# One step of the attention pipeline, three VectorE jobs in another order

## The chip, the cores and the metric

The kernel runs on one core of a Trainium2 chip. The metric is the device time of one execution in microseconds. Three runs of the kernel before took 2973.51, 2974.47 and 2975.86 us; the median is 2974.47.

## The reference, cut to what matters

The reference is four transformer layers on one sequence of 512 tokens, model width 1024, in float32: two layers of a first block and two of a second block. The change touches the second block alone. Each of its layers has two attentions over 8 heads of 64, computed in blocks of 128 queries:

```python
# fox_attention: causal, with a decay from summed forget gates
s = einsum('bhqd,bhkd->bhqk', qi, k) * scale + ci[..., :, None] - c[..., None, :]
p = softmax(where(kpos <= qpos, s, -inf)); o = einsum('bhqk,bhkd->bhqd', p, v)
# nsa_attention: compressed keys (o_c), selected keys (o_s), window keys (o_w), two groups of four heads
o_n = g[..., 0:1] * o_c + g[..., 1:2] * o_s + g[..., 2:3] * o_w
```

With 512 tokens the selection takes all key blocks, so o_s and o_w are two plain causal attentions with different keys and values. Around the attentions stand the projections of the layer (w_in, w_o_fox, w_o_nsa, w_out) and an MLP.

## The kernel before, in words

**Five programs.** Each engine has a program of its own, written by a function (`tensor_program`, `scalar_program`, `vector_program`, `sync_program`, `gpsimd_program`). They meet only at semaphores. An engine executes its instructions in the order in which its program issues them; nothing reorders them later.

**Weights.** They come in units of up to 128x1024. SyncE loads a unit into `RAW`, ScalarE copies its upper part into `Wh` (line 1412), VectorE subtracts to get the lower part `Wl` (line 2110), and TensorE multiplies with three products, upper by upper, upper by lower, lower by upper (lines 643 to 645). `Wh` and `Wl` are made two units ahead, at the moment when a program calls `next_unit`.

**Attention beside projections.** The attentions are generators ("sides"). The projection loops call `tick()` after each few matmuls, and each tick lets every open side do one step. All engine programs tick in the same places, so that step i of an attention stands at the same place of each program's order.

**A step.** The function `mixing` exists in the TensorE, ScalarE and VectorE programs. An item is one query block t of one head; there are 32 items in a fox layer and 64 in an nsa layer, 192 in all. Its scores are 128 rows by 128, 256, 384 or 512 columns. In step i:
- TensorE: `turn(i-3)` transposes item i-3's normalised exponents (line 858, waits for `norm`), then `head(i)` computes item i's scores (lines 921, 922, 924, 917), then, every second step, `mix` multiplies a pair with the values (lines 879, 880).
- ScalarE: `turn(i-3)` copies the turned exponents' upper part into `PTh` (line 1458), then `head(i)` takes the exponential with the sum (line 1592), which waits for item i's maximum.
- VectorE: `turn(i-3)` subtracts for the lower part `PTl` (`lower`, line 2158), which waits for ScalarE's upper part; `invert(i-1)` inverts a sum (line 2394), which waits for ScalarE's exponential of i-1; `head(i)` takes the maximum (line 2389), which waits for item i's scores.
- GpSimd: multiplies the exponents of an item by the inverse (line 3157), which waits for `invert`; TensorE's `turn` two steps later waits for this.

Every score tile and every turned tile has one of the 8 PSUM banks, handed out in rotation. A score's bank is free after the exponential, a turned tile's after VectorE's `lower`, an output's after `add_up` (lines 2854 and 2866), which follows a ScalarE copy (lines 1894, 1902) that stands behind the exponential of its step.

The evacuations of the projections (lines 2247, 2249, 2814, 3040) stand between the steps in VectorE's and ScalarE's order.

Of the kernel before, what the change touches and what calls it, by code (L numbers as in the profile page):

```python
# [586 lines left out]
def norm_of(block, l, place):  # L587
    return 4 * block + 2 * l + place
# [1501 lines left out]
def vector_program(ve, M, G, K, plan):  # L2090
# [63 lines left out]
    def lower(lo, src, h, gain=None):  # L2154

        ve.wait_ge(*hi.due())
        if gain is None:
            return ve.tensor_tensor(lo, src, h.bitcast(F32), ALU.subtract)  # L2158
        return ve.scalar_tensor_tensor(lo, src, gain, h.bitcast(F32), ALU.mult, ALU.subtract)  # L2159
# [222 lines left out]
    def mixing(B, group=False, add_up=None, finish=None, need=None, tail=7):  # L2382
        tag, items = B.tag, B.items

        def head(i):
            t, g, h = items[i]
            name = f"{tag} s{i}"
            ve.wait_ge(*K.full(name))
            ve.tensor_reduce(M.STT[:, 0, t, h:h + 1], M.bank[K.of(name)][:, 0:len(B.blocks(i)) * P], AX.X, ALU.max, negate=True).then_inc(*mx.up())  # L2389

        def invert(i):
            t, g, h = items[i]
            ve.wait_ge(*K.drained(f"{tag} s{i}"))
            ve.reciprocal(M.STT[:, 4, t, h:h + 1], M.STT[:, 1, t, h:h + 1]).then_inc(*rec.up())

        def turn(i):
            name = f"{tag} t{i}"
            lower(B.turned(M.PTl, i), M.bank[K.of(name)][:, 0:len(B.blocks(i)) * P].rearrange("p (k c) -> p k c", c=P),
                  B.turned(M.PTh, i)).then_inc(*K.empties(name))

        n = len(items)
        for i in range(n + tail):
            if group and i < n and (i == 0 or items[i][1] != items[i - 1][1]):
                while (tag, items[i][1]) not in done:
                    yield
            c = B.ended(i - 5)
            if need and c is not None and B.closes(c) and items[i - 5][0] in PAIRS[1]:
                while need not in done:
                    yield
            if 0 <= i - 3 < n:  # L2410
                turn(i - 3)
            if 0 <= i - 1 < n:
                invert(i - 1)
            if i < n:
                head(i)
            if c is not None and B.closes(c):
                done.add(B.outs[c])
            c = B.ended(i - 6)
            if c is not None and B.closes(c):
                add_up(*items[i - 6])  # L2420
            c = B.ended(i - 7)
            if finish and c is not None and B.closes(c):
                finish(*items[i - 7])
            yield
# [273 lines left out]
    for l in range(DEPTH):  # L2698
        n = norm_of(0, l, 0)
# [50 lines left out]
    for l in range(DEPTH):  # L2750
        n = norm_of(1, l, 0)
# [117 lines left out]
        def fox_side():  # L2869
            yield from idle(FOX_WAIT)  # L2870
            yield from mixing(fox_bundles(l), True, fox_sum, fox_out)
# [15 lines left out]
        def nsa_side():  # L2887
            while fox in sides.open:
                yield
            yield from blocks_side()  # L2890
            done.add(("blocks", l))
            while ("keys", l) not in done:
                yield
            q4 = M.QNS[:, :, :].rearrange("p a (h d) -> p a h d", d=64)
            tm = [M.RT[:, i, :].rearrange("p (a h b) -> p a h b", h=8, b=8) for i in range(4)]
            for s in range(NT):
                ve.wait_ge(*K.drained(f"qn{l} {s}"))
            rope(q4[:, :, :, 0:8], q4[:, :, :, 8:16], (over(nco, 8, 2), over(nsi, 8, 2), over(nsi, 8, 2), over(nco, 8, 2)), tm).then_inc(G.rq, 1)
            yield
            for j in range(2):  # L2900
                k4 = M.KST[:, :, j, :].rearrange("p a (h d) -> p a h d", d=64)
                tm = [M.RT[:, i, 0:64].rearrange("p (a h b) -> p a h b", h=2, b=8) for i in range(4)]
                if j == 0:
                    for s in range(NT):
                        ve.wait_ge(*K.drained(f"ks{l} {s}"))
                    ve.wait_ge(G.rq, l + 1)
                else:
                    ve.wait_ge(G.rk, 2 * l + 1)
                rope(k4[:, :, :, 0:8], k4[:, :, :, 8:16], (over(nco, 2, 2), over(nsi, 2, 2), over(nsi, 2, 2), over(nco, 2, 2)), tm).then_inc(G.rk, 1)
                yield  # L2910
            yield from idle(2)
            for j in range(6):
                yield from heads_side(j)
            yield from idle(5)
            yield from mixing(nsa_bundles(l), add_up=nsa_sum, need=("compressed", l), tail=6)
# [312 lines left out]
```

## Time and profile before

| what | us |
|---|---|
| median of three runs | 2974.47 |
| the profiled execution's own time | 2974.36 |
| its span, first to last instruction | 2972.6 |
| TensorE matmuls busy in it | 2786.2 (94%) |
| VectorE busy | 1497.9 (50%) |
| ScalarE busy | 1215.4 (41%) |
| GpSimd busy | 131.9 (4%) |
| mean granted TensorE clock | 0.973 of full |

Times in the profile are microseconds from the span's start, unless marked ns. A row that ends in [x <-Y] says that the engine sat idle for x before the instruction, until Y had ended. The steps of `mixing` lie in four stretches: fox about 1268 to 1385 and 2150 to 2270, nsa about 1434 to 1638 and 2316 to 2520.

### The profile page before, as it was taken

To read this page: it belongs to the slowest core of one execution; us is meant where nothing else is said; L and a number is where in the kernel's file an instruction comes from. 1 tells how busy PE (TensorE), PEld (TensorE's weight loads), DVE (VectorE), ACT (ScalarE), POOL (GpSimd) and SP (SyncE) were. 2 spreads that over 40 slices of the span, in tenths; PEclk is the share of its full clock that TensorE was granted. 3 is DMA by queue.
4 is the path that set the end of the run, shared out by engine and by line. 5 is a ranking of instruction groups with operands and counts; after the bars stand their busy time and mean duration, and the time that the engine had idled before them with its cause. 6 is when DMAs were issued, how large, how long until landed. Compare 5 with 4: busy or idle time off the path is not lost.

```text
span 2972.6 us, 34957 instructions
## 1 busy us (share of the span) xinstructions
PE 2786.2 (94%) x13625; PEld 2286.9 (77%) x13625; DVE 1497.9 (50%) x2695; ACT 1215.4 (41%) x2169; POOL 131.9 (4%) x221
## 2 busy tenths in 40 slices
PE   7999999998999999979889999999979888999998
PEld 6777888886778888767667888888767677888886
DVE  6755433357543434656655553343656655543343
ACT  4553222245432223455656343232445655342231
POOL 1000000000000000011111000000010111000000
PEclk9899999999999999989999999999989999999999
DMA  4102332330123323212211223332212211233332
GB/s 127 40 25 86 99 98 94 98 89 26 38 87 100 97 95 100 81 37 71 79 36 43 86 91 100 94 97 93 81 36 85 65 36 43 93 100 99 95 97 78
DMA packets 186359, 231.42 MB, mean 78 GB/s; under 512 B 11874, under 2 KB 140356, under 8 KB 186196
## 3 DMA queue, kind: packets, MB, share of 16 engines
q1 hardware_dynamic: 184500, 225.95, 24.2%
q0 software_dynamic: 976, 1.32, 0.3%
q8 instruction: 109, 1.79, 0.2%
q10 hardware_dynamic: 720, 1.92, 0.2%
q14 instruction: 54, 0.44, 0.0%
HBM read 227.05 MB, written 2.11 MB: 77 GB/s over the span
## 4 chain that ended last, share of the span: by engine, by line
PE 74%; DVE 13%; ACT 7%; issue 4%; DMA 0%; POOL 0%; ACTq 0%; DVEq 0%; SPq 0%; POOLq 0%
PE bank L643 22%; PE bank L645 22%; PE bank L644 22%; DVE Wl L2110 2%; ACT Wh L1412 2%; DVE PT L2158 2%; DVE STT L2389 1%; PE bank L803 1%; ACT P L1592 1%; ACT PT L1458 1%; PE bank L858 1%; PE bank L879 1%; PE bank L740 1%; DVE KAl L2814 1%; PE bank L1103 1%
## 5 line engine op out<-in xcount | busy, mean ns | idle before, releaser
L2110 DVE TENSOR_TENSOR Wl<-RAW,Wh 128x1024 fp32r<-128x1024 f32 (+3 forms) x434 | 511.2, 1200 | 396.3 <-ACT Wh L1412 395.4
L1412 ACT ACTIVATE Wh<-RAW 128x1024 fp32r<-128x1024 f32 (+3 forms) x434 | 438.1, 1032 | 367.9 <-PE bank L645 367.4
L643 PE MATMUL bank<-Hh,Wh 128*128 128x512 f32 (+1 forms) x976 | 395.5, 405 | 9.1 <-DVE Wl L2110 7.5
L645 PE MATMUL bank<-Hh,Wl 128*128 128x512 f32 (+1 forms) x976 | 385.2, 395 | 0.0
L644 PE MATMUL bank<-Hl,Wh 128*128 128x512 f32 (+1 forms) x976 | 385.0, 394 | 0.0
L643 PE MATMUL bank<-Wh,A 128*128 128x512 f32 x864 | 337.2, 390 | 0.0
L645 PE MATMUL bank<-Wh,A 128*128 128x512 f32 x864 | 336.2, 389 | 0.0
L644 PE MATMUL bank<-Wl,A 128*128 128x512 f32 x864 | 336.2, 389 | 0.0
L643 PE MATMUL bank<-HA,Wh 128*128 128x512 f32 x704 | 276.7, 393 | 7.2 <-DVE HA L2159 7.2
L645 PE MATMUL bank<-HA,Wl 128*128 128x512 f32 x704 | 275.5, 391 | 0.0
L644 PE MATMUL bank<-HA,Wh 128*128 128x512 f32 x704 | 275.3, 391 | 0.0
L643 PEld LDWEIGHTS bank<-Hh,Wh 128*128 128x128 f32 (+1 forms) x976 | 185.4, 190 | 50.2 <-DVE Wl L2110 8.4
L645 PEld LDWEIGHTS bank<-Hh,Wl 128*128 128x128 f32 (+1 forms) x976 | 184.4, 189 | 41.8
L644 PEld LDWEIGHTS bank<-Hl,Wh 128*128 128x128 f32 (+1 forms) x976 | 184.8, 189 | 34.9
L643 PE MATMUL bank<-Wh,Hh 128*128 128x512 f32 (+2 forms) x512 | 207.1, 405 | 4.3 <-DVE Wl L2110 2.7
L645 PE MATMUL bank<-Wh,Hl 128*128 128x512 f32 (+2 forms) x512 | 195.2, 381 | 0.0
L644 PE MATMUL bank<-Wl,Hh 128*128 128x512 f32 (+2 forms) x512 | 194.5, 380 | 0.0
L1592 ACT ACTIVATE P<-bank,STT 128x384 f32<-128x384 f32 (+1 forms) x192 | 101.4, 528 | 219.5 <-DVE STT L2389 219.3
L645 PEld LDWEIGHTS bank<-Wh,A 128*128 128x128 f32 x864 | 162.2, 188 | 33.7
L644 PEld LDWEIGHTS bank<-Wl,A 128*128 128x128 f32 x864 | 162.2, 188 | 33.3
L643 PEld LDWEIGHTS bank<-Wh,A 128*128 128x128 f32 x864 | 162.2, 188 | 33.3
L2158 DVE TENSOR_TENSOR PT<-bank,PT 128x384 fp32r<-128x384 f32 (+1 forms) x192 | 93.9, 489 | 169.2 <-ACT PT L1458 168.4
(371 smaller groups left out, 4440.8 us busy)
## 6 DMA issues: line engine op xcount, KB each, us to landing
RAW<-in_w_up_dram SPq DMA_DIRECT2D x108, 512.0 KB, 3.7
RAW<-in_w_down_dram SPq DMA_DIRECT2D x108, 512.0 KB, 3.8
RAW<-in_w_in_dram SPq DMA_DIRECT2D x90, 512.0 KB, 3.5
RAW<-in_w_gate_dram SPq DMA_DIRECT2D x44, 512.0 KB, 3.5
RAW<-in_w_out_dram SPq DMA_DIRECT2D x28, 512.0 KB, 3.8
RAW<-in_cmp_w_dram SPq DMA_DIRECT2D x16, 512.0 KB, 3.9
RAW<-in_w_o_fox_dram SPq DMA_DIRECT2D x8, 512.0 KB, 3.4
RAW<-in_w_o_nsa_dram SPq DMA_DIRECT2D x8, 512.0 KB, 3.4
```

Of the source, the lines that this page charges most:

```text
L643: pe.matmul(o, sh, mh, start=first, stop=False)
L644: pe.matmul(o, sh, ml, start=False, stop=False)
L645: return pe.matmul(o, sl, mh, start=False, stop=last)
L740: i = pe.transpose(b[:, s * P:(s + 1) * P], M.X[:, s, k * P:(k + 1) * P], ident)
L803: x = pe.matmul(b[:, h * 64:(h + 1) * 64], M.PT[:, i % 3, k * P:(k + 1) * P], values(g, h, kb[k]), start=k == 0, stop=k == len(kb) - 1)
L858: x = pe.transpose(b[:, k * P:(k + 1) * P], e[:, k * P:(k + 1) * P], ident)
L879: pe.matmul(b[:, c:c + w], v, ph, start=B.opens(n) and k == 0, stop=False, skip_group_check=True)
L1103: pe.matmul(b[:, 0:w], M.MQ[0:96, h, t * P:w], M.MK[0:96, h, 0:w], start=True, stop=True)
L1412: sc.activation(M.Wh[:, v % NHL, 0:n], M.RAW[:, v % NRAW, 0:n], ACT.Copy).then_inc(G.w_hi, 1)
L1592: sc.activation(e, M.bank[K.of(name)][:, 0:e.shape[1]], ACT.Exp, bias=M.STT[:, 0, t, h:h + 1], accum_out=M.STT[:, 1, t, h:h + 1]).then_inc ...
L2110: ve.tensor_tensor(M.Wl[:, v % NRAW, 0:n], M.RAW[:, v % NRAW, 0:n], M.Wh[:, v % NHL, 0:n].bitcast(F32), ALU.subtract).then_inc(G.w_lo, 1)
L2158: return ve.tensor_tensor(lo, src, h.bitcast(F32), ALU.subtract)
```

## The change

VectorE's `mixing` issues the three jobs of a step in another order. Before: lower part of item i-3, inverse of item i-1, maximum of item i. After: maximum of item i, inverse of item i-1, lower part of item i-3. Instructions, operands, waits and the other engines' programs stay as they are; both attentions of both layers of the second block use the function.

```diff
@@ vector_program, mixing, the loop over steps
             if need and c is not None and B.closes(c) and items[i - 5][0] in PAIRS[1]:
                 while need not in done:
                     yield
+            if i < n:
+                head(i)
+            if 0 <= i - 1 < n:
+                invert(i - 1)
             if 0 <= i - 3 < n:
                 turn(i - 3)
-            if 0 <= i - 1 < n:
-                invert(i - 1)
-            if i < n:
-                head(i)
             if c is not None and B.closes(c):
                 done.add(B.outs[c])
```

## Rows read from the trace of the kernel before

**Rows 1.** Windows: start:end, length, busy us (count), clock, DMA share, GB/s.

```profile
1434.00:1638.00 204.00, 173.72 (x993) 139.31 (x991) 107.84 (x277) 118.12 (x258) 38.98 (x64) 0.95 0.14 42
2150.00:2270.00 120.00, 98.13 (x530) 77.95 (x529) 67.62 (x144) 60.54 (x136) 19.53 (x32) 0.91 0.14 43
```

**Rows 2.** TensorE's waits, 1434 to 1638 (nsa): total us, times, longest.

```profile
PE bank L858 <- POOL P L3157: 13.2, 9, 2.7
PE bank L1285 <- DVE CB L2986: 5.2, 2, 3.3
PE bank L858 <- DVE ONS L2866: 4.4, 3, 2.0
PE bank L921 <- DVE PT L2158: 3.6, 3, 1.8
```

**Rows 3.** TensorE's waits, 2150 to 2270 (fox).

```profile
PE bank L858 <- POOL P L3157: 8.7, 2, 7.3
PE bank L879 <- DVE OAy L2854: 4.8, 2, 4.4
PE bank L858 <- DVE OAy L2854: 4.7, 1, 4.7
PE bank L921 <- DVE OAy L2854: 3.7, 3, 1.3
```

**Rows 4.** ScalarE's longest wait, 1434 to 1638.

```profile
ACT P L1592 <- DVE STT L2389: 68.0, 54, 2.7
```

**Rows 5.** The chain that ended last, by line, 1434 to 1638.

```profile
by line: issue 13.4%; DVE PT L2158 8.0%; DVE Wl L2110 6.3%; DVE STT L2389 6.0%; ACT Wh L1412 5.7%; ACT P L1592 5.3%; PE bank L643 5.1%; ACT PT L1458 4.9%; PE bank L645 4.6%; PE bank L644 4.5%; PE bank L858 3.5%; ACT L1592 3.5%; PE bank L879
```

**Rows 6.** One line's instructions each: durations ns min/median/max, starts, forms.

```profile
L2389 DVE TENSOR_REDUCE STT<-bank x192: 270/470/692, 1271.6 to 2516.3; 128x1 f32<-128x384 f32 x48, 128x1 f32<-128x512 f32 x48, 128x1 f32<-128x128 f32 x48, 128x1 f32<-128x256 f32 x48
L2158 DVE TENSOR_TENSOR PT<-bank,PT x192: 279/487/693, 1282.0 to 2520.0; 128x384 fp32r<-128x384 f32 x48, 128x512 fp32r<-128x512 f32 x48, 128x128 fp32r<-128x128 f32 x48, 128x256 fp32r<-128x256 f32 x48
L2394 DVE RECIPROCAL STT<-STT x192: 150/153/164, 1277.1 to 2518.1; 128x1 f32<-128x1 f32 x192
```

**Rows 7.** Timeline of an nsa step: start, duration, engine, line, operands, [idle <-releaser].

```profile
1483.18 0.23 PE L917 MATMUL bank<-CMB,IDB 128*128 128x128 bf16 x1
1483.26 0.60 ACT L1458 ACTIVATE PT<-bank 128x512 fp32r<-128x512 f32 x1 [0.88 <-PE bank L858]
1483.89 0.69 DVE L2158 TENSOR_TENSOR PT<-bank,PT 128x512 fp32r<-128x512 f32 x1 [0.44 <-ACT PT L1458]
1484.57 0.27 DVE L2389 TENSOR_REDUCE STT<-bank 128x1 f32<-128x128 f32 x1
1484.87 0.37 ACT L1592 ACTIVATE P<-bank,STT 128x128 f32<-128x128 f32 x1 [1.02 <-DVE STT L2389]
1486.93 0.33 PE L858 MATMUL bank<-CST,P 128*128 128x128 f32 x1 [1.55 <-DVE ONS L2866]
```

**Rows 8.** Timeline of a step behind a weight subtraction.

```profile
1465.93 1.23 DVE L2110 TENSOR_TENSOR Wl<-RAW,Wh 128x1024 fp32r<-128x1024 f32 x1 [1.77 <-ACT Wh L1412]
1467.07 0.68 DVE L2158 TENSOR_TENSOR PT<-bank,PT 128x512 fp32r<-128x512 f32 x1
1468.52 0.45 PE L858 MATMUL bank<-CST,P 128*128 128x128 f32 x1 [2.66 <-POOL P L3157]
```

**Rows 9.** Timeline around a fox output's wait.

```profile
1294.84 0.48 PE L921 MATMUL bank<-KAh,QA 128*128 128x512 f32 x1
1296.66 0.68 DVE L2249 SCALAR_TENSOR_TENSOR TQ<-bank,RBB 128x512 f32<-128x512 f32 x1
1299.74 0.67 DVE L2389 TENSOR_REDUCE STT<-bank 128x1 f32<-128x512 f32 x1
1302.48 0.58 PE L879 MATMUL bank<-PT,VF 128*128 128x256 f32 x1 [4.40 <-DVE OAy L2854]
```

**Rows 10.** ScalarE's exponentials ahead of the 4.7 us wait of the second fox stage.

```profile
2207.65 0.58 ACT L1592 ACTIVATE P<-bank,STT 128x384 f32<-128x384 f32 x1 [1.28 <-DVE STT L2389]
2210.83 0.69 ACT L1592 ACTIVATE P<-bank,STT 128x512 f32<-128x512 f32 x1 [1.02 <-DVE STT L2389]
```

## The prediction

> **What bounds the kernel now.** I read four views. The windows first, for the stretches in which the changed steps run [rows 1]: columns are TensorE matmul and weight load, VectorE, ScalarE and GpSimd busy. In the 204 us of an nsa stage TensorE is busy 173.7 us, VectorE 107.8 and ScalarE 118.1, and the granted clock is 0.95; in 120 us of a fox stage TensorE is busy 98.1 and the clock is 0.91. So TensorE is not full here, though it is 94% busy over the span, and the two other engines together are busy for about one stage length: they could do their work side by side easily, but if they take turns they fill the stage.
>
> The waits come second. TensorE waits in the nsa stage for GpSimd's multiply (13.2 us), for `add_up` (4.4), for a turned tile's bank (3.6) and for the compressed branch (5.2) [rows 2]; with five smaller groups (3.4 together) that is 29.8 us. In the fox stage it is 21.9 us [rows 3]. Both layers: about 103 us, of 2972.6.
>
> Third, who makes these late: ScalarE's exponential waits for VectorE's maximum 54 times in one nsa stage, 68.0 us in all, 1.26 us each [rows 4]. The chain of the stage [rows 5] confirms it: VectorE's lower part has 8.0% of it, 16.3 us, the maximum 6.0%, the exponential 5.3%, the upper part 4.9%. That is the taking of turns: upper part (ScalarE), lower part, inverse, maximum (VectorE), exponential (ScalarE), then whatever ScalarE has next. Elsewhere in the kernel the chain lies on matmuls, and this change does not reach it.
>
> **The change part by part.** Nothing is added or removed; 192 steps get another order on VectorE. No DMA is in these steps, and GpSimd, SyncE and TensorE keep their order. The medians are 0.47 us for the maximum, 0.49 for the lower part, 0.15 for the inverse, of which 0.07 passes before the next starts; for the same tile the maximum and the lower part cost nearly the same, 0.27 to 0.69 us [rows 6].
>
> (a) *The maximum goes ahead.* In the step of [rows 7] the scores' last matmul ends at 1483.41, ScalarE's upper part at 1483.86, and the maximum starts only at 1484.57, behind the lower part that waited for the upper one. In the new order the maximum runs 1483.45 to 1483.75, beside the upper part; the exponential follows the upper part at 1483.9 instead of 1484.87. That is 0.97 us less, and the ScalarE copy of the output, the next `Wh`, the `Wl` that waits for it, and `add_up` all come 0.9 us sooner. TensorE's wait of 1.55 us at 1486.93 would be about 0.65. This is a step in which VectorE keeps up with TensorE. Where VectorE is behind by a step, the whole idle time before the exponential (1.0 to 1.6 us) can go.
>
> (b) *Behind a `Wl`.* In [rows 8] VectorE comes from a weight subtraction and everything is ready. Before: lower part 0.68, inverse, GpSimd, transpose. After: maximum 0.67 in its place, then the inverse. The inverse gains nothing, and TensorE's 2.66 us wait shrinks only by what came before the `Wl`. Its exponential does gain the lower part and the inverse, 0.75 us.
>
> (c) *The lower part goes last.* It starts later by the maximum and the inverse, 0.47 + 0.07 = 0.54 us at the median, unless it had to wait for ScalarE anyway. Queued behind it are only the projection evacuations. Who waits for it: `mix`, two steps on, which has room, and the reuse of its PSUM bank. TensorE waited for that bank three times in the nsa stage, 3.6 us [rows 2]; I let all three grow by 0.54, 1.6 us per layer.
>
> (d) *The inverse behind the maximum.* Where a fox stage starts, TensorE waits 7.3 us for item 0 [rows 3]; item 0's inverse now stands behind item 1's 512-wide maximum, 0.67 us. TensorE waits that much more, but this does not set the later end: VectorE's and ScalarE's own order, which the 4.4 us wait hangs on, is not shifted. Price 0; 0.7 per layer if I am wrong.
>
> *The nsa stage summed.* I walked the chain from one matmul event to the next and gave each section either the amounts of (a) and (b) or the TensorE waits in it, whichever is less (they are the single entries of the groups in [rows 2]; times are ends of sections). To 1445: one step as in (a), 1.0. To 1468: waits of 1.1, 1.8 and 2.7; a `Wl` step's 0.75 on its way to the exponential, a step as in (a), and 0.5 at a 128-wide step, 2.2. To 1478: 0.2. From 1483 to 1502: no matmul at all in the chain, waits of 1.6, 1.7, 0.4 and 0.5 us, of which 3.5 can go. To 1527: 2.3, the rest being table loads of ScalarE, which stay. To 1543: 0.9. From there to 1638: 4.2 us of waits that hang on a step, take 3.2; the compressed branch's 5.2 us stay. Sum 13.3, below the 16.3 us that the lower part has in the chain. Minus (c), 1.6: 11.7 us per layer. The ends for this term: -1.6 (nothing of (a) arrives) and 24.6 (29.8 of waits less the 5.2).
>
> *The fox stage summed.* In [rows 9] the scores of 512 are issued at 1294.84, but VectorE reaches their maximum at 1299.74: it is a step behind. The projection's tile `TQ` is handled at 1296.66; with the two idle spans before it gone VectorE is free for it when TensorE has it, about 1295.0, which is 1.65 sooner; the 512-wide maximum then stands ahead of a 0.29 us lower part, so 1.95 us of the 4.40 us wait go. Before the 4.7 us wait two exponentials sit idle for 1.28 and 1.02 us [rows 10], both in steps where VectorE is behind: 2.3 us. The three waits of about 1.2 us for a score's bank [rows 3] lie in steps where the maximum has to wait for the scores anyhow: 0. Sum 4.2 us per layer. Ends: -0.7 (d), and 9.1, the two waits.
>
> *The clock.* At 0.95 and 0.91 the two stretches lose some 10 us each to a granted clock below full [rows 1], and the matmuls behind a wait run at the lower of the two levels. The waits shrink by 15.9 of 51.7 us, a third; a third of the 20 us would be 6, but part of it lies where TensorE waits anyway. I take 1.4 us per layer, ends 0 and 6.
>
> Sum: 2 x (11.7 + 4.2 + 1.4) = 34.6 us. The profiled execution took 2974.36, which is the median of the runs (2974.47) within 0.1, so the forecast is 2940.
>
> A rule that speaks against all of this: the Trainium skill, page "Perfetto Trace Analysis", section "Identifying the Most-Contended Engine", says to find the engine with the highest occupancy and to work on that one first. By it TensorE at 94% is the engine, VectorE at 50% is not, and a reordering on VectorE is worth 0. The trace bears it out for the span, not for these stretches, where TensorE's share is 82 to 85%.
>
> **The rivals.**
> *No change (2974).* TensorE is the bound, and each wait that goes comes back at the next table load, `Wl` or bank. For it: 94% busy; ScalarE's table loads and the `Wl` steps of (b), where the inverse gains nothing. Against: 68 us of exponentials waiting in one stage, and a chain that leaves TensorE for 18 us at a time.
> *Half of it (2958).* The waits for GpSimd, 13.2 us of the 29.8, hang on the inverse, which (b) does not speed up; if most of these steps start with a `Wl` the nsa term is about 5 and the fox term 2: 2 x (5 + 2 + 0.7) = 15 to 16 us.
> *More (2918).* Once ScalarE and VectorE work side by side they never fall behind, and nearly all step waits go: 2 x (20 + 6 + 2) = 56.
> *Slower (2980).* The maximum waits for scores, and VectorE is in order: while it waits, a ready inverse and a ready lower part stand behind it. Where TensorE is itself held at the scores for a bank (PT, ONS, OAy, P: 3 + 3 + 3 + 1 times per layer or so), the bank it wants next comes free later by 0.54 us or more, and so on at each such place. It decides if VectorE is seldom behind TensorE. 10 places x 0.54 x 2 layers = 11, less a few us of (a): +6. Against it: 54 of the 64 exponentials of an nsa stage waited for the maximum [rows 4], and in [rows 7, 9] the scores were there first.
> *It doesn't do what it says.* The order in a step could be masked by the waits themselves: if the scores always landed later than the lower part ended, old and new would be the same. Against it: [rows 7, 9] show scores that lay ready; this is part of "no change".
>
> **Chances.** Forecast (2926 to 2951) 0.57, half of it 0.17, more 0.12, no change 0.07, slower 0.07. The likeliest gives 2940. The range reaches to the half case and most of the "more" case: 2920 to 2965. A measurement of this kernel tells 0.2%, about 6 us, from no change. Faster by over that: 0.85, same 0.08, slower 0.07.
>
> **What would show it.** Right: ScalarE's wait for the maximum falls from 68 us in an nsa stage to under 25; the chain's share of the lower part falls from 8% to under 3%; TensorE's waits for GpSimd and `add_up` in the nsa stage fall from 17.6 to under 9; the 4.4 and 4.7 us waits of fox to about 2.4 each; the 7.3 us wait grows to about 8. The first block and the MLPs keep their times. Wrong: TensorE's waits for PT's bank grow past 6 us per nsa stage, or VectorE sits idle before the maximum for scores longer than ScalarE sat before, or the clock of the stretches stays and eats the gain.

## The result and the profile after

The changed kernel took 2933.7 us (median of four runs, 2932.05 to 2935.11) against 2973.99 for the kernel before (2973.43 to 2975.86): ratio 0.9863, 95% interval 0.9846 to 0.9880, 40.3 us less. The profiled execution took 2932.05 us with a span of 2930.2, 42.4 us less than the span of before; it was the fastest of the four runs. The same 34957 instructions ran; TensorE's matmuls were busy 2775.1 us (95%), VectorE 1503.6 (51%), ScalarE 1216.8 (42%).

Where in the kernel it was gained is read from instructions that both traces have. The first block ends within 0.3 us of before. The first transposes of nsa's queries (line 932) mark the end of the fox stage, and the sums split for the output projection (`MXl`, line 2158, first and last of 16) come behind the nsa stage of either layer. One line from each kernel's record of line 932, the kernel before first; the two times in each are those of the first and the last start:

```profile
L932 PE MATMUL bank<-CST,QNS x32: 270/272/329, 1405.3 to 2299.0; 128*128 128x128 f32 x32
```

```profile
L932 PE MATMUL bank<-CST,QNS x32: 270/272/328, 1398.8 to 2271.0; 128*128 128x128 f32 x32
```

At 1405.3 the changed kernel is 6.5 us ahead, at 2299.0 28.0 us. Line 2158 of the kernel before, then of the changed one:

```profile
L2158 DVE TENSOR_TENSOR MXl<-M,MXh x16: 691/693/694, 1664.3 to 2568.6; 128x512 fp32r<-128x512 f32 x16
```

```profile
L2158 DVE TENSOR_TENSOR MXl<-M,MXh x16: 692/693/693, 1642.7 to 2526.3; 128x512 fp32r<-128x512 f32 x16
```

Here it is 21.6 and 42.3 us ahead. So the four stages gave 6.3 (fox), 15.1 (nsa), 6.5 (fox) and 14.3 us (nsa), and nothing came from elsewhere.

The stretches of the changed kernel as windows, columns as in [rows 1]: nsa of layer 0, fox of layer 1. Each reaches some 4 to 6 us further into the work than its window in [rows 1], so it holds more matmuls.

```profile
1427.00:1622.00 195.00, 176.61 (x1026) 143.00 (x1025) 113.11 (x282) 121.71 (x263) 39.18 (x64) 0.96 0.16 47
2128.00:2246.00 118.00, 100.32 (x549) 80.56 (x548) 72.06 (x147) 63.13 (x139) 19.57 (x32) 0.94 0.15 49
```

TensorE is busy for 91% of the nsa window, where it was 85% in [rows 1]; with the end of the window moved to the same work (1427.4 to 1616.8, 995 matmuls, 171.0 us busy) it is 90%. Its waits there, the answer to [rows 2]:

```profile
PE bank L858 <- POOL P L3157: 8.0, 4, 3.4
PE bank L1285 <- DVE CB L2986: 4.2, 2, 2.5
PE bank L921 <- DVE PT L2158: 3.2, 3, 1.9
PE bank L858 <- DVE ONS L2866: 1.7, 2, 1.2
```

GpSimd's 13.2 us became 8.0 and `add_up`'s 4.4 became 1.7. The turned tile's bank stayed near its 3.6. In the fox stage, the answer to [rows 3]:

```profile
PE bank L858 <- POOL P L3157: 8.1, 1, 8.1
PE bank L921 <- DVE OAy L2854: 3.7, 3, 1.3
PE bank L858 <- DVE OAy L2854: 3.1, 1, 3.1
PE bank L879 <- DVE OAy L2854: 2.8, 1, 2.8
```

The start of the stage waits 8.1 us instead of 7.3, the two output waits fell from 4.7 and 4.4 to 3.1 and 2.8, the three short ones did not move. ScalarE's waits of the nsa stage, the answer to [rows 4], and VectorE's:

```profile
ACT P L1592 <- DVE STT L2389: 34.8, 38, 2.7
ACT PT L1458 <- PE bank L858: 32.8, 21, 4.5
```

```profile
DVE STT L2389 <- PE bank L917: 29.8, 19, 5.2
DVE Wl L2110 <- ACT Wh L1412: 18.3, 15, 2.5
DVE PT L2158 <- ACT PT L1458: 11.4, 14, 1.6
```

The exponential's wait for the maximum halved, from 68.0 us to 34.8. What is new is that ScalarE's upper part waits for TensorE's transposes (32.8 us, 15.3 before), and VectorE's maximum for TensorE's scores (29.8 us; no such wait was in the trace of before). Both engines are now up with TensorE in more of the steps and wait for it there. The chain of the same window, the answer to [rows 5]:

```profile
by line: issue 9.9%; PE bank L643 9.1%; PE bank L645 8.2%; PE bank L644 8.1%; PE bank L858 5.4%; DVE Wl L2110 5.2%; DVE STT L2389 4.9%; ACT Wh L1412 4.5%; PE bank L879 3.6%; ACT P L1592 3.5%; PE bank L921 3.0%; PE bank L880 2.9%; PE bank L9
```

The lower part (8.0% in [rows 5]) is no longer among the lines shown, the last of which has 2.9%; the three matmul lines have 25.4% where they had 14.2% (24.7% with the window ended at 1617, at the same work).

The step of [rows 7], in the changed kernel:

```profile
1472.27 0.23 PE L917 MATMUL bank<-CMB,IDB 128*128 128x128 bf16 x1
...
1472.35 0.60 ACT L1458 ACTIVATE PT<-bank 128x512 fp32r<-128x512 f32 x1 [2.10 <-PE bank L858]
...
1472.54 0.29 DVE L2389 TENSOR_REDUCE STT<-bank 128x1 f32<-128x128 f32 x1
...
1472.86 0.37 ACT L1592 ACTIVATE P<-bank,STT 128x128 f32<-128x128 f32 x1
1472.98 0.69 DVE L2158 TENSOR_TENSOR PT<-bank,PT 128x512 fp32r<-128x512 f32 x1
...
1474.92 0.33 PE L858 MATMUL bank<-CST,P 128*128 128x128 f32 x1 [0.45 <-DVE ONS L2866]
```

The maximum runs while ScalarE still makes the upper part. From the upper part's start to the exponential's start it is 0.51 us; in [rows 7] it was 1.61. TensorE's wait for the output behind it is 0.45 us instead of 1.55. The step of [rows 8], behind a `Wl`:

```profile
1455.74 1.23 DVE L2110 TENSOR_TENSOR Wl<-RAW,Wh 128x1024 fp32r<-128x1024 f32 x1 [2.02 <-ACT Wh L1412]
1456.88 0.68 DVE L2389 TENSOR_REDUCE STT<-bank 128x1 f32<-128x512 f32 x1
1457.48 0.15 DVE L2394 RECIPROCAL STT<-STT 128x1 f32<-128x1 f32 x1
...
1458.34 0.30 PE L858 MATMUL bank<-CST,P 128*128 128x128 f32 x1 [3.41 <-POOL P L3157]
```

From the start of `Wl` to TensorE's transpose it is 2.60 us, 2.59 in [rows 8]: the maximum took the lower part's place, and the wait grew from 2.66 to 3.41 because TensorE came to it earlier. The exponential, though, started 1.86 us behind the start of `Wl` instead of 2.52. Three waits of this kind (2.0, 3.4 and 1.7 us) are most of what is left of GpSimd's 8.0.

The gain can be split once more. Between the same instructions of both traces (borders at 1270.8, 1405.3, 1664.3, 2152.0, 2299.0 and 2568.6 before, at 1270.6, 1398.8, 1642.7, 2130.5, 2271.0 and 2526.3 after; what lies between the third and the fourth border belongs to no stage), TensorE's waits can be summed, and its busy time can be compared, as the number of matmuls is the same to within one:

| stage | gain, us | TensorE's waits, before and after | TensorE busy, before and after |
|---|---|---|---|
| fox, layer 0 | 6.3 | 21.9, 17.6 | 111.5, 109.4 |
| nsa, layer 0 | 15.1 | 33.5, 21.5 | 226.2, 223.2 |
| fox, layer 1 | 6.5 | 23.1, 18.9 | 124.0, 121.7 |
| nsa, layer 1 | 14.3 | 31.0, 20.4 | 238.2, 234.5 |

The waits shrank by 31.1 us and the busy time by 11.1, together the 42.2 us of the four stages. Over the whole kernel the busy time fell by the same 11.1 us (2786.2 to 2775.1) for 13625 matmuls in both, and the mean granted clock rose from 0.973 to 0.977. So about a quarter of the gain is TensorE doing the same work faster; that this is the clock, and not partly the modelled ends of single matmuls, is an estimate that the clock's mean supports.

### The profile page after: what moved, and what is told of

Same layout as the page of the kernel before. It is cut to its first block, busy times and chain, and to the rows that moved or that the text cites. A ratio compares the mean times of both kernels' runs of the same rounds, so it can differ in the third digit from the quotient of the medians.

```text
span 2930.2 us, 34957 instructions
## 1 busy us (share of the span) xinstructions
PE 2775.1 (95%) x13625; PEld 2282.6 (78%) x13625; DVE 1503.6 (51%) x2695; ACT 1216.8 (42%) x2169; POOL 132.2 (5%) x221
## 3 DMA queue, kind: packets, MB, share of 16 engines
q1 hardware_dynamic: 184500, 225.95, 24.7%
## 4 chain that ended last, share of the span: by engine, by line
PE 79%; DVE 11%; ACT 5%; issue 4%; DMA 0%; POOL 0%; DVEq 0%; ACTq 0%; SPq 0%
PE bank L643 23%; PE bank L645 23%; PE bank L644 23%; DVE Wl L2110 2%; PE bank L803 1%; PE bank L858 1%; ACT Wh L1412 1%; DVE STT L2389 1%; PE bank L879 1%; PE bank L740 1%; DVE KAl L2814 1%; PE bank L880 1%; PE bank L921 1%; PE bank L1103 1%; PE bank L788 1%
## 5 line engine op out<-in xcount | busy, mean ns | idle before, releaser
L643 PEld LDWEIGHTS bank<-HA,Wh 128*128 128x128 f32 x704 | 133.1, 189 | 36.9 <-DVE HA L2159 8.6
L645 PEld LDWEIGHTS bank<-HA,Wl 128*128 128x128 f32 x704 | 133.0, 189 | 27.7
```

The lines of the kernel that those rows point to most:

```text
L643: pe.matmul(o, sh, mh, start=first, stop=False)
L645: return pe.matmul(o, sl, mh, start=False, stop=last)
```

## The experiments

All were timed beside the kernel before on the same chip: 2975.40 us for the first four, 2973.98 for the next four, 2974.49 for the last four. Theory A says that the gain is the maximum's: that job no longer stands behind the lower part, so that ScalarE and VectorE work side by side. Its first rival says that it is the inverse's, because GpSimd's multiply and TensorE's transposes hang on it.

### Inverse ahead, maximum still last

```diff
+            if 0 <= i - 1 < n:
+                invert(i - 1)
             if 0 <= i - 3 < n:
                 turn(i - 3)
-            if 0 <= i - 1 < n:
-                invert(i - 1)
             if i < n:
                 head(i)
```

> VectorE's order is inverse of i-1, lower part of i-3, maximum of i: the inverse alone has left the lower part behind, the maximum still stands last. Theory A (the gain came from the maximum no longer waiting for the lower part, so that ScalarE's exponential runs beside VectorE): little, 2968 to 2974 us, and ScalarE's wait for the maximum stays near 219 us. Rival B (the gain came from the inverse and so from GpSimd's multiply, for which TensorE waited 43.6 us before and 32.2 after): most of the 40 us, 2935 to 2945.

Measured: 2975.1 us, ratio 0.9998 (0.9989 to 1.0007): no gain, and 1 us above theory A's range. Who waited for GpSimd's multiply in this kernel:

```profile
  PE bank L858: 30.5, 11
```

and how long ScalarE's exponential sat idle for the maximum:

```profile
  DVE STT L2389: 214.1, 172
```

TensorE's wait for GpSimd fell from 43.6 us in all to 30.5, below the 32.2 of the changed kernel, and the time did not move. The biggest wait in TensorE's list was shortened by 13 us for nothing: other waits grew, the one for a fox output (line 858, from 9.4 to 11.8 us) and the one for a turned tile's bank (line 921, from 6.3 to 9.6) among them, and all of TensorE's waits together are 168.9 us against 170.3. The exponential's wait stayed at 214 us (219 before), and so did the time. The rival falls.

### Maximum first, inverse last

```diff
+            if i < n:
+                head(i)
             if 0 <= i - 3 < n:
                 turn(i - 3)
             if 0 <= i - 1 < n:
                 invert(i - 1)
-            if i < n:
-                head(i)
```

> VectorE's order is maximum of i, lower part of i-3, inverse of i-1: the maximum first, the inverse last. Theory A: most of the gain, 2934 to 2944 us; the inverse comes a lower part (0.48 us) later than in the changed kernel, TensorE's wait for GpSimd is 35 to 45 us instead of 32.2, and ScalarE's wait for the maximum is near the changed kernel's 122 us. Rival B: the gain is gone, 2968 us or more.

Measured: 2935.2 us, ratio 0.9870 (0.9855 to 0.9885). TensorE's wait for GpSimd is 40.8 us, nearly the 43.6 of before, and the exponential's wait is 123.3. With the one above this is the whole test: the inverse's place is worth nothing or up to 1.5 us, the maximum's place is worth 39 to 40.

### Inverse, maximum, lower part

```diff
+            if 0 <= i - 1 < n:
+                invert(i - 1)
+            if i < n:
+                head(i)
             if 0 <= i - 3 < n:
                 turn(i - 3)
-            if 0 <= i - 1 < n:
-                invert(i - 1)
-            if i < n:
-                head(i)
```

> VectorE's order is inverse of i-1, maximum of i, lower part of i-3. Theory A: at least the gain of the changed kernel, and the wait at the start of each fox stage (8.0 us in the changed kernel) back to 7.3, as the inverse no longer stands behind a 512-wide maximum: 2928 to 2933 us. Rival C (the inverse waits for ScalarE's exponential, now that ScalarE runs beside VectorE, and holds back the maximum behind it; in the changed kernel it waited 12 times, 8.8 us): 2936 to 2945.

Measured: 2932.0 us (2931.2 to 2932.3), ratio 0.9854 (0.9840 to 0.9869). The interval holds the changed kernel's ratio, so it is the same within what can be told. The start of the fox stage is back at 7.3 us, and the output's wait follows it; TensorE's instructions in that stage of layer 0:

```profile
1277.81 0.88 PE L858 MATMUL bank<-CST,P 128*128 128x128 f32 x3 [7.33 <-POOL P L3157]
...
1300.30 0.39 PE L879 MATMUL bank<-PT,VF 128*128 128x256 f32 x1 [2.88 <-DVE OAy L2854]
```

At the second the changed kernel stood at 1302.25. The 2 us were given back before the stage ended: line 932 starts at 1398.74 here and at 1398.79 in the changed kernel. Most of that is the clock: behind the next output wait (3.42 us, ended at 1325.48) the granted clock was at the lower level until 1329, behind the changed kernel's (3.08 us, ended at 1327.09) it was not, and TensorE was 1.6 us ahead before and level at 1339. In layer 1, where the clock fell in both, this order ends the stage 0.8 us sooner (2270.2 against 2271.0). Rival C's mechanism is there (the inverse waited for the exponential 74 times, 37.5 us, against 12 times and 8.8 us), but it does not lengthen anything: the maximum behind it waited that much less for its scores (67.7 us against 103.4), and the two waits together are 105.2 us against 112.2.

### Fox alone, nsa alone

```diff
+            if tag[:3] == "fox":       # "nsa" in the other kernel
+                if i < n:
+                    head(i)
+                if 0 <= i - 1 < n:
+                    invert(i - 1)
+                if 0 <= i - 3 < n:
+                    turn(i - 3)
+            else:
...
```

> The new order in the two fox attentions only, the old one in the nsa attentions. By the changed kernel's trace the fox stages gave 6.2 and 6.5 us: 2961 us. By the forecast's term (2 x 4.2, and at most 1.4 of clock): 2965. If the fox stage's start (0.7 us more of waiting per layer) were carried to the end, 2967 or more.

> The new order in the two nsa attentions only. By the changed kernel's trace (15.1 and 14.4 us): 2946 us; by the forecast's terms (11.7 + 1 of clock, twice): 2950. With the fox-only kernel's 9 us the two would add up to the whole 40 if nothing passes from one stage to the next.

Measured: fox alone 2966.1 us, ratio 0.9968 (0.9958 to 0.9978), 9.3 us less than before; nsa alone 2940.4, ratio 0.9885 (0.9871 to 0.9900), 33.6 us less. Together 42.9, against 40.3 for the whole change: the stages add up within the scatter of these runs (about 3 us). The trace had read 12.7 and 29.4, and nsa alone gave more than either expected time; why 3 to 4 us lie on the other side of the border was not shown. The clock can be a part of it: in the profiled execution of fox alone TensorE is busy 2786.6 us, as long as before, so that no part of the 11.1 us came with it, and in that of nsa alone 2776.0.

### One more VectorE job in each step, in either order

```diff
         def turn(i):
             name = f"{tag} t{i}"
+            t, g, h = items[i]
+            ve.wait_ge(*hi.now_next())
+            ve.wait_ge(*own.now())
+            ve.tensor_reduce(M.STT[:, 3, t, h:h + 1], M.bank[K.of(name)][:, 0:len(B.blocks(i)) * P], AX.X, ALU.max).then_inc(*own.up())
             lower(B.turned(M.PTl, i), ...
```

> The order of the kernel before, with one VectorE job more in every step, directly ahead of the lower part and released by the same upper part: a maximum over the turned tile into a column that nothing reads (0.47 us at the median, 192 times, 90 us of VectorE work). It doubles what stands between ScalarE's upper part and the maximum. Theory A (the old order has the lower part in the chain): it is paid in most nsa steps and in the fox steps where VectorE is behind, 40 to 80 us more, 3015 to 3055 us. If VectorE had idle time to hide it (rival D: its busy share is 50%): under 10 us more.

> The changed kernel with the same extra job ahead of the lower part, which is now last in the step. Theory A: the job lies beside ScalarE's exponential and is hidden in the steps that wait for scores; it is paid only where the chain runs through VectorE's next work (a weight subtraction, an evacuation, a bank): 10 to 30 us more, 2944 to 2964 us, and the distance between this and the old order with the extra job grows from 40 to 60 or more. Rival E (the change gained only by a lucky placement, the lower part being as dear in the new order): as much more as in the old order.

Measured: in the old order 3042.4 us, ratio 1.0229 (1.0213 to 1.0244), 68.4 us more than before; in the new order 2957.0, ratio 0.9941 (0.9927 to 0.9956), 23.3 us more than the changed kernel. The 192 jobs are some 90 us of work. An amount equal to three quarters of it was paid in the old order and to one quarter in the new. Not all of that is waiting: between the profiled executions TensorE's busy time for its 13625 matmuls grew by 35.7 of the 71.4 us in the old order (mean granted clock 0.962 against 0.973) and by 10.1 of 23.5 in the new. In the old order the clock thus took, by this estimate, about half of what the job cost. The change is worth 85 us to a kernel with the extra job, 40 without. This is the strongest support for the account by place: what stands between the upper part and the maximum is mostly in the chain, what stands behind the maximum is mostly not. That VectorE is busy for half of the time hid little of it.

### ScalarE's step turned round as well

```diff
 # scalar_program, mixing, on top of the changed kernel
-            if 0 <= i - 3 < n:
-                turn(i - 3)
             if i < n:
                 head(i)
+            if 0 <= i - 3 < n:
+                turn(i - 3)
```

> The changed kernel, and ScalarE's step turned round too: exponential of item i first, then the upper part of i-3. Theory A says that the two engines must have something to do beside each other: the upper part now waits until scores and maximum are there, instead of running beside them, and the lower part behind it comes later; 5 to 20 us slower than the changed kernel, 2939 to 2954. If the exponential's wait were all that matters (rival F: each time the exponential starts sooner the stage is shorter): 2925 to 2932.

Measured: 3009.0 us, ratio 1.0114 (1.0097 to 1.0131): 75 us slower than the changed kernel and 35 slower than before. The sign is as expected, the size is not. Now the upper part waits for scores, maximum and exponential, and VectorE's lower part behind it. VectorE's idle time ahead of the lower part in this kernel, and then who waited for the lower part:

```profile
  ACT PT L1458: 201.7, 184
```

```profile
  PE bank L921: 30.7, 34
...
  PE bank L858: 10.7, 11
```

In the changed kernel the first of these is 25.7 us in 34 places, and TensorE's wait for PT's bank at line 921 is 6.3 us in 6 places. The bank is free late, and TensorE waits for it ahead of the next scores or transposes. The two engines are back at taking turns as well: ScalarE's exponential waits for the maximum 296.5 us with the upper part behind it (122.2 in the changed kernel), and VectorE waits for that upper part with the next maximum behind it. This is the kind of loss that the slower rival of the prediction named, brought about on the other engine: an in-order engine that waits for scores with ready work behind it. On VectorE the change was harmless in this respect, since TensorE's wait for that bank at line 921 stayed at 6.3 us. Which of the two, the bank or the turns, has the larger share of the 75 us was not separated.

### `Wl` behind the first step

The walk of [rows 8] leaves one loss in place: at the start of a weight unit VectorE stands at `Wl`, which waits for ScalarE's `Wh`, with the step behind it. While a side is open, these kernels make the newest unit's part after the next tick.

```diff
-    def next_unit():
-        u = unit[0]
-        unit[0] += 1
-        while cut[0] <= min(u + AHEAD, len(plan) - 1):
+    def cut_to(m):
+        while cut[0] <= min(m, len(plan) - 1):
...
+    def next_unit():
+        u = unit[0]
+        unit[0] += 1
+        cut_to(u + AHEAD - bool(sides.open))
+        return unit_of(plan, u)[0]
+
+    def tick():
+        sides.tick()
+        cut_to(unit[0] - 1 + AHEAD)
```

The first has it on VectorE with the changed order; the second on ScalarE too; the third on VectorE with the order inverse, maximum, lower part; the fourth on VectorE with the old order.

> The changed kernel, and while an attention or another side is open VectorE makes the lower part of the next weight unit (Wl, 1.22 us, line 2110) behind the first step of the unit instead of ahead of it. Theory G (what is left of the chain is VectorE standing at Wl, which waits for ScalarE's Wh, with a maximum behind it): the maximum runs beside Wh, 5 to 20 us faster than the changed kernel, 2914 to 2929 us, ScalarE's wait for the maximum under 100 us instead of 122. Rival H (Wl two units ahead has no room, or the new place holds back evacuations): TensorE waits for Wl, 2936 to 2955.

> As the one before, and ScalarE's upper part Wh (0.96 us) is also behind the first step of the unit. Theory G: the exponential and the upper part of the step come 1 us sooner on ScalarE as well, but the room between Wh, Wl and TensorE shrinks by a step: 2912 to 2932 us. Rival H: worse than Wl alone by 5 us or more, as Wh waits for a buffer that is free late and then Wl and the second step wait behind it.

> Wl behind the first step, and VectorE's step in the order inverse, maximum, lower part. If the small gain of that order (2932.0 against 2933.7) is real and adds up: 1 to 4 us less than Wl later alone. If the inverse, waiting for the exponential, stands ahead of the maximum more often now that nothing else stands there: 0 to 4 us more.

> Wl behind the first step, with the old order lower part, inverse, maximum. Theory G with A: the old order's turns stay, so only a part of what Wl later gives is had: 2960 to 2970 us. If the Wl ahead of the step was what made the old order slow, nearly all of the 40 us come here too: 2925 to 2940.

| kernel | us | ratio (95%) |
|---|---|---|
| `Wl` later, changed order | 2912.1 | 0.9787 (0.9772 to 0.9802) |
| `Wl` and `Wh` later | 2938.3 | 0.9872 (0.9853 to 0.9890) |
| `Wl` later, inverse first | 2914.2 | 0.9793 (0.9778 to 0.9807) |
| `Wl` later, old order | 2963.4 | 0.9960 (0.9945 to 0.9975) |

`Wl` later is 21.6 us faster than the changed kernel, 2 us beyond the range of theory G, 62 us faster than before, and the fastest of the study. Its exponentials wait for the maximum:

```profile
ACT P L1592 <- DVE STT L2396: 100.0, 111, 3.4
```

(122.2 us in the changed kernel; the expectation had said under 100), and of TensorE's waits

```profile
PE bank L858 <- POOL P L3164: 18.5, 15, 5.5
PE bank L643 <- DVE Wl L2108: 14.4, 3, 5.8
```

the one for GpSimd fell from 32.2 to 18.5, while that for `Wl` grew from 10.2 to 14.4. In the old order the same edit gives 11.1 us, half: each edit is worth more with the other there (40.3 alone and 11.1 alone, 62.4 together), as is to be expected where either shortens the same chain of turns. Moving `Wh` as well loses 26 us against `Wl` alone, beyond what theory G allowed and of the size that rival H gave; TensorE waits for GpSimd 29.3 us again. Rival H's mechanism is not shown by that: ScalarE's wait ahead of `Wh` did not grow (360.4 us against 363.5), while VectorE's for `Wh` ahead of `Wl` did, from 316.3 to 381.8 us. Which of the later `Wh`'s effects costs the time was not separated. The inverse first gave no more here: 2914.2 against 2912.1 us, intervals that overlap.

## Why the prediction was right

The forecast was 34.6 us less (2940), the runs gave 40.3, inside the range and in the band of the forecast case. The mechanism was right: the maximum left its place behind the lower part, and TensorE's waits shrank by about what was forecast for them. One term, the clock, was much too small, and within the two terms of waits misses cancelled, which is luck. By its steps:

(a) *The maximum ahead.* Right in kind and size: 0.97 us was forecast for the step of [rows 7], and the trace of after has 1.10 less from upper part to exponential. That it is the maximum's place and not the inverse's is shown by the two permutations: 0 us without it, 39 to 40 with it alone.

(b) *Behind a `Wl` nothing for the inverse.* Right to 0.01 us (2.59 and 2.60); the exponential there gained 0.66 of the 0.75 us. What stayed in such steps was worth 21.6 us more once `Wl` moved.

(c) *The bank of the lower part.* Too dear: 1.6 us per layer was set for it. The nsa stage's waits for it went from 3.6 to 3.2 us, and the 6.3 us of the whole kernel at line 921 are 6.3 still. In the step of [rows 7] the lower part starts 0.63 us behind the upper part's start in both traces, as ScalarE set its start before too; it idled for ScalarE in 121 of 192 steps before and in 34 after.

(d) *The start of fox.* TensorE waits 0.7 us more, as forecast. That this does not set the later end, price 0, is not decided: the order with the inverse first takes the 0.7 us away and ends the stage level in layer 0, where the clock differed, and 0.8 us sooner in layer 1. The changed kernel in layer 0 also paid in clock: behind the longer start the lower level lasted until 1284.8, in the kernel before until 1281.7.

*The nsa term.* 11.7 us per layer was forecast, as waits that go, and TensorE's waits fell by 12.0 and 10.6. Here two misses cancelled: the 1.6 us of (c) were not lost, and of the 13.3 that were to be gained about as much less came.

*The fox term.* 4.2 us per layer were forecast, and the waits fell by 4.3 and 4.2, but not where they were put. The two output waits shrank by 1.6 each, where 1.95 and 2.3 were forecast; a second wait for GpSimd, 1.35 us at 1323.10 in the kernel before, went too and was not in the sum; the start took its 0.7 back. The right total is luck.

*The clock.* This is the term that was mis-sized: 1.4 us were set for a whole layer, and TensorE's busy time fell by 5.1 us in layer 0 and 6.0 in layer 1. These 11.1 us instead of 2.8 are what lies between the forecast of 34.6 and the 42.4 us of the trace; the waits fell by 31.1 where 31.8 were forecast. TensorE's windows from the second output wait to the end of the fox stage of layer 0, before and after:

```profile
1330.00:1406.00 76.00, 70.42 (x373) 0.96 0.20 63
```

```profile
1327.00:1399.50 72.50, 67.53 (x373) 1.00 0.21 66
```

The same 373 instructions with the same waits of 1.1 to 1.3 us took 3.3 us less, because the granted clock was at the lower level for the first 6 us of the one and for nothing of the other. The shorter wait is not enough to explain it: in layer 1 of the same trace the wait at that place is as short (3.07 us), and the clock was low behind it until 2189.3. The stretch gave 0.9 us there (0.97 and 0.98), so this is a gain that comes or not.

*The rivals.* "No change" had 94% busy on its side, and with it the rule that the prediction took from the Trainium skill, page "Perfetto Trace Analysis", section "Identifying the Most-Contended Engine". That section does name the engine with the highest occupancy as the first to work on, but it also says that TensorE's headroom is to be judged by other measures than its matmul busy share, one of them the busy share of its weight loads, which was 77% over the span. "Worth 0" was the prediction's own step, and the runs decide against it: a reordering on an engine at 50% gave 40 us. The same page's "Optimization Strategy" goes on to look for the gaps of the chosen engine within a stage and for what they wait for; read so it agrees with this case, where TensorE was busy for 85% of the nsa stage and its gaps shrank by 12.0 us. "Slower" named a kind of loss that VectorE's new order did not bring (the waits for PT's bank at line 921 stayed at 6.3 us); turning ScalarE's step brought one like it, 75 us together with the turns.

The thresholds named beforehand were too strict twice: the exponential's wait in an nsa stage fell to 34.8, not under 25, and TensorE's waits for GpSimd and `add_up` to 9.7, not under 9. The lower part's share of the chain (under 3%) and the start of fox (8.1) were met; the output waits were to be about 2.4 and are 3.1 and 2.8. None of the signs of being wrong came: PT's bank 3.2 us, VectorE idle before the maximum 29.8 us where ScalarE had been for 68.0.

## What to carry to other kernels

Two engines that each are busy for half of the time can still set a stage's length if their jobs release each other in turn; look at who waits for whom on the idle engines, and put first in each step the job that releases the other engine, last the job that was itself just released by it. A shortened wait is no gain by itself: 13 us less of TensorE's largest wait gave 0, since TensorE waited as long in all, at other places. To see whether a job is in the chain, add a second one beside it: the time grew by 76% of its cost in one order and by 26% in the other. And compare TensorE's busy time for the same matmuls before and after: here a quarter of the gain lay there and not in the waits.

## What the runs showed of the hardware

In layer 0 of the kernel before, the granted clock fell to the lower of its two levels (1.2 and 2.4 GHz) during a wait of TensorE of 4.71 us and stayed there for some 6 us of work behind it (512-column matmuls started 0.43 us apart). Behind the wait of 3.08 us at the same place in the changed kernel it stayed at the higher level (0.23 us apart). With the wait shorter by 1.6 us, the work behind it took 3.3 us less.

The length of such a wait did not settle what the clock did. Behind waits of 2.82 us at one place (line 879, the first fox output), with dense matmuls before, it was at the lower level for 3.4 us in the changed kernel, for 6.8 us in layer 0 of fox alone, which runs the same fox stage, and for nothing in layer 1 of the kernel with the maximum first and the inverse last. Behind waits of 3.07 to 3.10 us at the next place it was low for 3.4 us three times (layer 1 of the changed kernel, both layers of fox alone) and not at all once.

Over the whole kernel TensorE's busy time for the same 13625 matmuls was 2775.1 us in the changed kernel, 2786.2 before and 2821.9 with the extra job in the old order, at mean granted clocks of 0.977, 0.973 and 0.962. No run changed the clock alone, so that its share of each stage stays an estimate from these figures.
